# Norms with column statistics in a two-block transformer kernel, and small transfers moved from ScalarE's to GpSimd's queue

## The reference

```python
def rms_norm(x, g):
    y = x * lax.rsqrt(jnp.mean(x * x, axis=-1, keepdims=True) + 1e-6)
    return y * g

# first block, per layer l: mod = silu(c) @ w_ada[l] + b_ada[l]
h = rms_norm(x, norm1_g[l]) * (1 + sc1) + sh1      # norm "n1"
x = x + g1 * token_mixer(h, ...)                   # gated linear attention + differential attention
h = rms_norm(x, norm2_g[l]) * (1 + sc2) + sh2
x = x + g2 * hier_moe(h, ...)                      # 32 experts, top 2

# second block, per layer i
h  = rms_norm_2(x, norm_g[i, 0]) * (1 + sc1) + sh1         # norm "nA"
hc = rms_norm_2(ctx, norm_g[0, 0]) * (1 + csc1) + csh1     # norm "ctx", layer 0 only
y  = attention_mixers(h, hc, ...) if i == 0 else fourier_mix(h) @ w_f
x  = x + g1 * rms_norm_2(y, norm_g[i, 1])                  # norm "pA"
h  = rms_norm_2(x, norm_g[i, 2]) * (1 + sc2) + sh2         # norm "ffn"
x  = x + g2 * rms_norm_2(conv_ffn(h, ...), norm_g[i, 3])   # norm "pF"
```

## Time and profile before

| | |
|---|---|
| runs | 2394.58, 2396.43, 2398.36 us; median 2396.43 |
| the profiled execution | 2398.32 us, of which the profile's span is 2396.5 |
| PE | busy 2164.7 us, 90% of the span |
| DVE, ACT, POOL | 42%, 28%, 11% |
| the chain that ended last | PE 83%, DVE 10%, ACT 3%, others 4% |
| mean granted clock of TensorE | 0.959 of 2.4 GHz |

### The profile page before, as it was taken

One profiled execution on the slowest core, in us unless ns is written; L12 is line 12 of the kernel. 1 busy time (PEld: TensorE's weight loads), 2 busy tenths in 40 slices (PEclk: granted clock), 3 DMA queues, 4 the chain that ended last, 5 costly groups with the idle time before them and its releaser, 6 DMA issues.

```text
span 2396.5 us, 31356 instructions
## 1 busy us (share of the span) xinstructions
PE 2164.7 (90%) x13461; PEld 1541.3 (64%) x13461; DVE 1004.1 (42%) x1904; ACT 672.7 (28%) x1192; POOL 271.7 (11%) x116
## 2 busy tenths in 40 slices
PE   4998988999999989899899999998989799887998
PEld 2776674555555467777455555555756699866997
DVE  2465541111111136564221111112435677656776
ACT  2334421101111043343221111011023555434553
POOL 1453420000000044453000000000000000000000
PEclk7999989999999989999999999999999899998998
DMA  9865669999999966567799999997436365323550
GB/s 324 292 217 176 253 239 370 409 409 409 409 409 409 385 233 220 200 229 289 294 366 409 409 409 409 409 409 273 158 131 228 101 216 188 103 73 122 180 194 18
DMA packets 251189, 657.88 MB, mean 275 GB/s; under 512 B 16800, under 2 KB 129278, under 8 KB 238627
## 3 DMA queue, kind: packets, MB, share of 16 engines
q1 hardware_dynamic: 244032, 652.27, 72.0%
q10 hardware_dynamic: 7011, 3.53, 0.5%
HBM read 654.70 MB, written 1.06 MB: 274 GB/s over the span
## 4 chain that ended last, share of the span: by engine, by line
PE 83%; DVE 10%; ACT 3%; SPq 1%; issue 1%; DMA 1%; ACTq 0%
PE ps L407 82%; DVE AR L1898 2%; DVE AR L740 1%; DMA ring<-in_w_in 1%; SPq L340 1%; DVE AR L1945 1%; DVE xT L2515 1%; DVE hT L2513 1%; DVE XLr L802 1%; ACT AR L765 0%; ACT HBr L385 0%; ACT AR L726 0%; DVE ARr L1579 0%; DVE AR L793 0%; ACT hTr L774 0%
## 5 line engine op out<-in xcount | busy, mean ns | idle before, releaser
L407 PE MATMUL ps<-ring,AR 128*64 128x512 f32 (+1 forms) x2032 | 524.9, 580 | 33.1 <-DVE AR L1945 33.1
L407 PE MATMUL ps<-XLr,HBr 128*128 128x256 f32 x1408 | 417.8, 297 | 64.5 <-DVE XLr L802 44.9
L407 PE MATMUL ps<-AR 128*128 128x128 f32 (+6 forms) x2088 | 379.7, 344 | 14.0 <-DVE AR L1879 7.5
L407 PEld LDWEIGHTS ps<-ring,AR 128*64 128x64 f32 (+1 forms) x2032 | 203.1, 140 | 273.1 <-issue 266.7
L407 PE MATMUL ps<-hTr,ringr 128*128 128x256 f32 x1280 | 371.9, 291 | 0.0
L407 PE MATMUL ps<-hTr,HBr 128*128 128x256 f32 x1280 | 371.4, 290 | 0.0
L391 POOL TENSOR_TENSOR ringr<-ring,HBr 128x1024 fp32r<-128x1024 f32 x112 | 271.5, 2440 | 853.0 <-ACT HBr L385 853.0
L407 PEld LDWEIGHTS ps<-AR 128*128 128x128 f32 (+2 forms) x2088 | 288.8, 191 | 119.6 <-issue 76.9
L407 PEld LDWEIGHTS ps<-XLr,HBr 128*128 128x128 f32 x1408 | 279.1, 198 | 88.9 <-issue 38.8
L385 ACT ACTIVATE HBr<-ring 128x1024 fp32r<-128x1024 f32 x260 | 266.1, 1050 | 238.8 <-PE ps L407 211.2
L407 PEld LDWEIGHTS ps<-hTr,ringr 128*128 128x128 f32 x1280 | 256.0, 200 | 0.8 <-issue 0.5
(11 more groups left out here) (270 smaller groups left out, 2362.5 us busy)
## 6 DMA issues: line engine op xcount, KB each, us to landing
ring<-in_w_expert_in SPq DMA_DIRECT2D x154, 1024.0 KB, 15.2
ring<-in_w_expert_out SPq DMA_DIRECT2D x84, 1024.0 KB, 10.1
ring<-in_mod_w SPq DMA_DIRECT2D x48, 1024.0 KB, 6.6
ring<-in_ffn_w_up SPq DMA_DIRECT2D x44, 1024.0 KB, 5.7
ring<-in_w_in SPq DMA_DIRECT2D x40, 1024.0 KB, 5.5
ring<-in_w_ada SPq DMA_DIRECT2D x40, 1024.0 KB, 7.3
HB<-in_w_expert_in SPq DMA_DIRECT2D x36, 1024.0 KB, 14.5
XL<-in_w_expert_in SPq DMA_DIRECT2D x22, 1024.0 KB, 14.3
```

The costliest lines, as they stand in the source:

```text
L407: return pe.op.matmul(out_, lhsT, rhs, start=start, stop=stop, **kw)
```

## The change

- Every `NormMod` and `PostNorm` gets a helper `Rstd`. TensorE now takes the chunk of squares as weights and one column of 1/1024 as moving operand: 16 products of one column give the mean of each token in a 128x2 tile (tokens in partitions). ScalarE's root and VectorE's reciprocal work on 128x2. VectorE makes two 128x128 diagonal matrices of it (`diag`), and one product with a matrix of ones (`pe_spread`) spreads it over 128x256 in PSUM, from where VectorE reads it.
- `NormMod`: the scale by the spread value comes first (`dve_scale`); `coef` and shift are both applied by ScalarE's one instruction. VectorE's order for split norms is scale k, then low k-3, the last three lows after all.
- `PostNorm`: squares are taken of PSUM in four instructions of 512 columns, the copies to `hT` are gone, the spread value is copied to SBUF, and the add of chunk k-1 stands behind the scale of chunk k.
- The 31 late small transfers stay behind each other, but in GpSimd's queue (`pool_small`), ahead of all of its low parts. They wait until the sixth chunk of the first modulation weights has landed. One transfer (`act_table`) stays with ScalarE.
- The q/k weights of layer 1 (`sp_mixer_first`) and the context's key/value weights (`sp_kv(sp, 0)`) are loaded ahead of the flag at the end of a layer's experts, the order of slots in `all_` is changed for it, and two high parts of layer 1 are made before the last expert pair ends.
- `pe_heads` starts with the context's keys, then the norm's statistics, the context's values, the spread, and the q projections, which now wait chunk by chunk.
- The context norm's spread stands behind the second pair's down product.

The diff, cut to this:

```diff
         def pool_program(pool):
+            pool_small(pool)
             for name, of, k, w, sel, by in units:
                 if by == "pool":
                     low_part(pool, name, of, k, w, sel, pool_lo)
...
-        def act_small(act):
+        def act_table(act):
             act.wait_ge(*dve_pro["tab"])
             act.op.dma_start(scr, tab).then_inc(*q_scr.inc("all"))
-            act.wait_ge(*dve_pro["cleared"])
+
+        def pool_small(pool):
+            pool.wait_ge(*dve_pro["cleared"])
+            pool.wait_ge(*mod_in[5]["all"])
             def some(dst, src):
-                act.op.dma_start(dst, src).then_inc(*q_sml.inc("all"))
+                pool.op.dma_start(dst, src).then_inc(*q_sml.inc("all"))
...
+        class Rstd:
+            def pe_stats(self, pe):
+                pe.wait_ge(*self.banks.turn("norm", self.tag))
+                b = self.banks["norm", self.tag]
+                for k in range(8):
+                    pe.wait_ge(*act_norm[self.squared(k)])
+                    for j in range(2):
+                        a = k * 256 + j * 128
+                        t = mm(pe, b[:, j:j + 1], self.sq[:, a:a + 128], C("m1024", 0, 1), k == 0 and j == 0, k == 7,
+                               skip_group_check=True)
+            def act_root(self, act):
+                act.wait_ge(*pe_norm[self.tag, "mean"])
+                act.op.activation(self.st, self.banks["norm", self.tag][:, 0:2], ACT.Sqrt, bias=eps[:, 0:1])
+            def dve_diagonal(self, dve):
+                dve.wait_ge(*act_norm[self.tag, "root"])
+                dve.op.reciprocal(self.st, self.st).then_inc(*dve_norm.inc())
+                for j in range(2):
+                    dve.op.tensor_scalar(diag[:, j * 128:(j + 1) * 128], ident, self.st[:, j:j + 1], None, ALU.mult)
+            def pe_spread(self, pe):
+                pe.wait_ge(*dve_norm[self.tag, "diagonal"])
+                mm(pe, self.rs, C("ones"), diag[:, :], True, True).then_inc(*pe_norm.inc(self.tag, "spread"))
...
             def act_apply(self, act):
+                act.wait_ge(*dve_norm[self.tag, "coef"])
                 for k in range(8):
                     act.wait_ge(*dve_norm[self.tag, "scaled", k])
-                    act.wait_ge(*dve_mod[self.mod])
-                    act.op.activation(self.full[:, sl(k)], self.full[:, sl(k)], ACT.Identity,
+                    act.op.activation(self.full[:, sl(k)], self.full[:, sl(k)], ACT.Identity, scale=self.coef[:, k:k + 1],
                                       bias=self.shift[:, k:k + 1]).then_inc(*act_norm.inc(self.tag, "out", k))
...
+            def dve_scale(self, dve, low=True):
+                dve.wait_ge(*pe_norm[self.tag, "spread"])
                 for k in range(8):
-                    dve.op.scalar_tensor_tensor(self.full[:, sl(k)], self.src[:, sl(k)], self.coef[:, k:k + 1], self.rs,
-                                                ALU.mult, ALU.mult).then_inc(*dve_norm.inc(self.tag, "scaled", k))
-                    if self.split and k:
-                        self.dve_low(dve, k - 1)
+                    dve.op.tensor_tensor(self.full[:, sl(k)], self.src[:, sl(k)], self.r.rs, ALU.mult)
+                    if self.split and low and k >= 3:
+                        self.dve_low(dve, k - 3)
...
-            all_ = ((8, 9, 10, 7, 5, 6, 0, 1, 2, 3, 4, 12, 13), (8, 9, 11, 6, 7, 5, 0, 1, 2, 3, 12, 13, 4))[l]
+            all_ = ((8, 9, 10, 7, 5, 6, 1, 2, 3, 4, 0, 12, 13), (8, 9, 11, 6, 7, 5, 2, 3, 12, 13, 0, 1, 4))[l]
...
+            if l == 0:
+                sp_mixer_first(sp, 1)
+            else:
+                sp_kv(sp, 0)
             sp.wait_ge(*dve_moe["flag", l])
...
                 if (l, p) == (1, 1):
-                    normC.pe(pe)
+                    normC.r.pe_stats(pe)
                 pe_turn(pe, l, m, p)
                 pe_down(pe, l, m, p)
+                if (l, p) == (1, 1):
+                    normC.r.pe_spread(pe)
...
         def pe_heads(pe, m, norm):
-            pe.wait_ge(*norm.done(7))
             pe.wait_ge(*act_norm["ctx", "out", 7])
-            pe_projq(pe, 0, 0)
-            pe_projq(pe, 0, 1)
-            pe_projkv(pe, 0, 0)
+            pe_projkv_half(pe, 0, 0, 0)
+            norm.r.pe_stats(pe)
+            pe_projkv_half(pe, 0, 0, 1)
+            norm.r.pe_spread(pe)
+            pe_mods(pe, 2)
+            pe_projq(pe, 0, 0, norm)
+            pe_projq(pe, 0, 1, norm)
...
-            def act(self, act):
-                act_squares(act, self.tag, lambda k: hT[:, sl(k)], 8, 256, self.sq, self.ready)
-                act_root(act, self.tag, 256, self.rs)
+                for p in range(4):
+                    act.wait_ge(*self.summed(p))
+                    act.op.activation(self.sq[:, sl(p, 512)], self.y(p)[:, :], ACT.Square).then_inc(*act_norm.inc(self.tag, "sq", p))
+                self.r.act_root(act)
...
                 for k in range(8):
-                    y, x = hT[:, sl(k)], xT[:, sl(k)]
-                    dve.op.scalar_tensor_tensor(y, y, self.coef[:, k:k + 1], self.rs, ALU.mult, ALU.mult).then_inc(*dve_norm.inc())
-                    dve.wait_ge(*dve_norm.now())
-                    dve.op.tensor_tensor(x, x, y, ALU.add).then_inc(*dve_norm.inc(self.tag, "x", k))
+                    dve.op.scalar_tensor_tensor(self.sq[:, sl(k)], self.y(k // 2)[:, sl(k % 2)], self.coef[:, k:k + 1], self.rs, ALU.mult,
+                                                ALU.mult).then_inc(*dve_norm.inc(self.tag, "scaled", k))
+                    if k:
+                        self.dve_add(dve, k - 1)
+                self.dve_add(dve, 7)
```

More of the change, by code:

```diff
@@ L805, in done @@
             def done(self, k):
-                return dve_norm[self.tag, "low", k] if self.split else act_norm[self.tag, "out", 7]
+                return dve_norm[self.tag, "low", k] if self.split else act_norm[self.tag, "out", k]
         def act_halves(act, tag, hi, src, ready, n=8):
@@ L2181, in attention_bufs, with sp_kv @@
             return m
+        def sp_kv(sp, which):
+            W = A["attn_w_in_2"][0]
+            for n in range(2):
+                a = 1024 + which * 512 + n * 256
+                load(sp, ("akv", which, n), by_rows(W[:, a:a + 256]), 8, 256)
         def sp_attention(sp):
```

223 lines of the change are left out of this document (127 added, 96 removed).

## The result

| | median us | runs |
|---|---|---|
| before | 2397.22 | 4, from 2394.58 to 2398.36 |
| after | 2378.53 | 4, from 2372.16 to 2380.68 |

The ratio is 0.9919, 95% interval 0.9898 to 0.9940: 18.7 us faster, where the prediction had 39 us. The profiled execution of after has a span of 2378.9 us; mean granted clock 0.955 (before 0.959).

What follows compares the result with a forecast made beforehand. TensorE's waits, almost all at norms, were taken as the bound. Terms 0 + 10.4 - 1.4 + 9.2 + 13.2 + 3.7 + 3.8 = 38.9 off 2398.3, less 1.9, gave 2357.4 us; range 2341 to 2384.

Steps and rivals of the forecast that it cites:

- What bounds the kernel: Whole kernel: TensorE is busy in 90% of the span, so time is gained only where it waits, almost always at norms.
- Part 1: Norm n1 of layer 0 and the small transfers moved to GpSimd, at 1.0 us an issue: 0 us.
- Part 2: Norm n1 of layer 1: earlier squares, statistics of 4.1 us and a faster split apply; gain 10.4 us.
- Part 3: Context norm: TensorE waits at the spread for root, reciprocal and diagonals; loss 1.4 us.
- Part 4: nA and the heads: the context's keys and values fill both of TensorE's waits; gain 9.2 us.
- Parts 5 and 7: pA and ffn, two layers: gain 13.2 us, mostly split apply; granted clock behind three split norms: gain 3.8 us.
- Part 6: pF with the next nA, and pF of layer 1: copies dropped and pairs faster; gains 2.35 and 1.35 us.
- rival B: Start: all GpSimd issues slow; 2.35 us each eats all other gains, 3 us gives 2417; chance 6%.
- the own case: GpSimd issues of 0.71 to 1.42 us, with bounds on the heads' and clock's gains: 2343 to 2371 us; chance 70%.
- A: Start: GpSimd's issues of transfers with many short pieces much slower, a loss of 28 us: 2383 to 2387; chance 12%.
- C: Split norms: the apply's chain does not break, VectorE and ScalarE still wait in turn: 2377 us; chance 7%.
- D: Start: first low parts really on VectorE, so TensorE doesn't wait for GpSimd: 2346 us; chance 5%.

Runs made afterwards that it cites:

- b_small_pool: Kernel before with one part of the change alone, the 31 small transfers issued by GpSimd: 2398.57 us, ratio 1.0009 to before.
- a_means: Changed kernel with the norms' statistics, root and reciprocal in the old form (8 products of 256 columns), without diagonals, spread and its copy: 2366.43 us.
- a_wide: Changed kernel with each statistics product streaming 128 columns of 1/1024 instead of one: 2358.65 us, ratio 0.9843.
- b_lag3: Kernel before with only VectorE's low parts in split norms moved to three chunks late: 2365.30 us, ratio 0.9867.
- a_again: Changed kernel without any edit, timed and profiled once more: 2377.71 us.
- a_heads0: Changed kernel with the old order of the heads, norm and q ahead of the context's keys and values: 2372.77 us.

## Why the prediction was half right

- **What bounds the kernel**: right. All that moved lies at the norms.
- **Part 1, 0 us**: the stretch gained 5.9, for a reason that the sum hadn't. An issue (taken at 1.0, measured 0.57) was cheaper than all three of its candidates, by which the part's own formula gives its bound of 54, a gain of 8.4; and it didn't matter: undoing the move costs nothing. The step that failed is "So the unit ends at 23.7 + 31 d + 2.4 [...] = 31.2 + 31 d, or at 54 if that is later". It ended at about 57, set by the landing at 46.28 and ScalarE's queue behind it. The gain is the apply itself: all scales were done ahead of it, so it ran at 0.80 a chunk where the old took 1.70. No run has this alone, but the transfers alone leave the stretch at 183.9 (b_small_pool), and without the new statistics it stays at 178.1 (a_means). I had priced that pace in parts 2 and 5 and not here. The Trainium skill (DMA: Bandwidth & Descriptors, section "SWDGE vs HWDGE vs iDMA") says that software makes GpSimd's descriptors; the trace agrees, the page of after lists a queue `software_dynamic` with 1184 packets and the page of before none. But the 1.2 us an issue that I had estimated from that page's latencies was twice what the trace has; ScalarE's 31 issues took 0.71 each.
- **Part 2, 10.4**: 3.7 up to the last low part (33.96 us behind the experts' end, before 37.62), and with the clock behind it 6.0. The statistics took 6.98 us at the low clock and not 4.1 (2.9), the spread 1.2 and not 0.71 (0.5), and one low part 2.02 and not 0.42 (1.6), behind GpSimd's. They also began late: at 842.81, 3.0 us behind the start of the squares, where the sum had 0.4. TensorE had then been idle for 3.58 us (3.63 in a_wide, 3.66 at the heads); what holds it there no view shows.
- **Part 3, a loss of 1.4**: right; the lead over before went from 9.17 to 8.01 us there, 1.2.
- **Part 4, 9.2**: 3.9, of which 1.3 were lost in the attention. Keys 8.63 and values 8.84 instead of 7.07 each are 3.3 of the 5.3, and the start is 1.5 more: 1644.16, which is 1652.2 if one adds the 8.0 us by which the experts end earlier than before, where the sum had 1650.7. The keys were cold from the wait ahead of them, which the rows of q before (17.01 for two halves) had shown; I counted that gain for q and didn't charge keys with the same.
- **Parts 5 and 7, 6.6 and 1.9 a norm pair**: 4.7 and 3.8. The apply gained what was said (7.5 us, from 1869.75 to 1877.25, for 12.4; b_lag3 shows 7.8 and 8.4 with the clock's share, for which I had 5.2 + 1.9). The clock behind it came back as part 7 has it, and sooner: 1.00 from 1877 on, where before had 0.50 and then 0.84 over the 8 us behind the apply. The statistics took it back: 5.46 and a tail of 2.4 us behind the last square, where the sum had 4.1 and a small gain, and two spreads of 1.19 for 0.71.
- **Part 6, 2.35 and 1.35**: a loss of 2.5, and 1.0. Both norms in the first have statistics (5.03 and 6.99 us) and neither has a split apply that would gain. ScalarE's coefficient column took another 0.74.
- **The sums**: three figures don't follow from their own terms. Part 4's gives 9.4, 3 us an issue under rival B 2419, and the own case with all upper bounds 2375. None changes the account.
- **The rivals**: none came. A and B priced GpSimd's issues, C the apply's chain, D a reading of the name. The mechanism that halved the gain had no rival: that the new statistics themselves lower the clock.

The step behind parts 2, 4, 5 and 6 is one: "the router's four of that kind stand as 8 records in 1.03 us, 0.26 each, so 4.1 us". The size is right for the full clock, 3.63 in the heads. But I carried a duration over from a place with a full clock (1.00 at 336.2 to 337.3) to places where TensorE has waited, and no term had the clock fall through the norm itself. Part 7 looked at it only behind the split apply, from TensorE's busy share. Over the whole kernel that share rose from 90 to 92%, and the mean clock fell from 0.959 to 0.955. With 128 columns in the same products and nothing else changed, 19 us came back. That a_wide stands near the forecast's 2357.4 is luck in part: its first stretch gains 5.9 for 0, and its heads 7.2 for 9.2. The Trainium skill (TensorE: Matmul & The Clock Gate, section "Part 1: The HAM clock gate (the "warmup" mystery)") ties the clock to how busy TensorE has been; here a stretch with 5.46 of 6 us busy went at 0.66, so the busy time of these records did not keep it up.

The coefficient column was in reach too: the Trainium skill (ScalarE: Activation LUTs, section "What ACT_TABLE_LOAD costs") says that each per-partition pointer operand adds about 93 ns. The traces agree, 4.04 - 3.30 = 0.74 us for eight, 0.093 each.

## What to carry to other kernels

When a chain passes over three engines chunk by chunk, first let the last step run a few chunks late: here that order alone was worth 32 us, and the new arithmetic around it cost 12. A form of a product that looks cheaper wasn't cheaper here, where it streamed few columns: read the granted clock over it and behind it, and price it at the low level wherever TensorE has just waited. A transfer or an issue that is moved to another queue is worth only what the wait that ends last behind it allows; find that wait first.

## What the runs showed of the hardware

- The granted clock over a norm differed with the columns that TensorE streamed, at the same waits and nearly the same length of a product (32 records in 3.63 us with one column and 3.85 with 128, at the full clock): statistics of 1, 32, 64 and 128 columns gave 2377.7, 2376.1, 2364.9 and 2358.7 us, and one column 0.66, then 0.50, against 1.00, then 0.92, with 128 over pA.
- With one column the fall came at different points of the same code: the statistics of pA took 5.46 us in after, 5.52 in a_again and 3.75 in a_heads0.
- Keeping it up with unread products through two norms (1.00) was followed by 0.63 and 0.90 in the work behind. The kernel lost 12 us, of which the trace shows 0.6 in that stretch.
- An issue on GpSimd took 0.50 to 0.92 us, 0.57 on average; for the router weights 0.91 to 0.92, for which ScalarE's took up to 4.98.
- While GpSimd runs a low part, VectorE's operations with two operands in SBUF last up to 2 us longer (8 columns: 1.70 us for 0.16), and those that read one of them from PSUM don't (four in 1.41 us). The Trainium skill (GPSIMD Engine Reference, section "1. Specifications") names this contention for instructions with two SBUF inputs; the traces agree and give its price, the rest of GpSimd's instruction.
